# A gated FFN with a convolution over time: gate and up computed with tokens stationary instead of weights stationary

## The reference

```python
D_FF = 5632
def conv_ffn(h, w_up, conv_w, conv_b, w_down):
    s = h.shape[1]
    u = h @ w_up                                   # 256 x 2048 times 2048 x 11264
    u_pad = jnp.pad(u, ((0, 0), (CONV_WIDTH - 1, 0), (0, 0)))
    u = sum(conv_w[j] * u_pad[:, j:j + s] for j in range(CONV_WIDTH)) + conv_b
    gate, up = jnp.split(u, 2, axis=-1)
    return (jax.nn.silu(gate) * up) @ w_down       # 256 x 5632 times 5632 x 2048
```

## Time and profile before

| | |
|---|---|
| median of 3 runs | 2358.61 us |
| span of the profiled execution (its time less what lies around the span) | 2357.3 us |
| TensorE busy | 2348.9 us |
| VectorE busy | 1523.7 us |
| ScalarE busy | 1222.5 us |
| GpSimd busy | 364.5 us |
| HBM read | 446.54 MB, 190 GB/s over the span |

### The profile page before, as it was taken

How to read it: one execution, slowest core, us unless ns; L and a number is a source line. 1 busy time by engine, 2 the same in 40 slices (tenths; PEclk the granted TensorE clock), 3 DMA queues, 4 the chain that set the end, 5 groups by cost and what they waited for, 6 DMA issues and landing times.

```text
span 2357.3 us, 30238 instructions
## 1 busy us (share of the span) xinstructions
PE 2348.9 (100%) x11538; PEld 1988.3 (84%) x11538; DVE 1523.7 (65%) x1807; ACT 1222.5 (52%) x1598; POOL 364.5 (15%) x612
## 2 busy tenths in 40 slices
PE   9999999999999999999999999999999999999999
PEld 7998888888888888888877888888888888888887
DVE  6777865677567657667666676766655564565564
ACT  6555555555455445445565665655543443453442
POOL 0221410000000000000000445534231121130110
PEclk9999999999999999999999999999999999999999
DMA  9566786565655655655655767667676776766774
GB/s 307 166 188 178 162 218 210 166 189 183 210 179 184 208 180 185 208 180 179 223 191 164 212 196 220 200 213 218 199 222 202 198 212 206 203 207 206 204 217 150
DMA packets 310610, 468.10 MB, mean 199 GB/s; under 512 B 22577, under 2 KB 152241, under 8 KB 309825
## 3 DMA queue, kind: packets, MB, share of 16 engines
q1 hardware_dynamic: 291920, 440.52, 60.5%
q0 software_dynamic: 18016, 25.37, 5.0%
q10 hardware_dynamic: 528, 0.27, 0.1%
HBM read 446.54 MB, written 2.10 MB: 190 GB/s over the span
## 4 chain that ended last, share of the span: by engine, by line
PE 99%; DVE 0%; DMA 0%; SPq 0%; ACT 0%; issue 0%; POOL 0%; DVEq 0%
PE main L618 95%; PE aux L618 3%; PE aux L631 0%; DMA RAW<-in_w_in 0%; DVE LO L1260 0%; DVE AR L1263 0%; DVE XT L1263 0%; SPq L562 0%; PE aux L717 0%; SPq L575 0%; SPq L577 0%; PE aux L693 0%; DVE AR L1260 0%; ACT HI L864 0%; PE aux L641 0%
## 5 line engine op out<-in xcount | busy, mean ns | idle before, releaser
L1260 DVE TENSOR_TENSOR LO<-RAW,HI 128x1024 fp32r<-128x1024 f32 (+2 forms) x836 | 1011.4, 1229 | 630.2 <-ACT HI L864 604.0
L864 ACT ACTIVATE HI<-RAW 128x1024 fp32r<-128x1024 f32 (+2 forms) x836 | 853.6, 1043 | 684.2 <-PE main L618 586.0
L618 PE MATMUL main<-HI,XT 128*128 128x512 f32 (+1 forms) x2496 | 766.0, 385 | 2.6 <-DVE LO L1260 2.6
L618 PE MATMUL main<-HI,YT 128*128 128x512 f32 x2240 | 692.4, 389 | 0.0
L618 PEld LDWEIGHTS main<-HI,XT 128*128 128x128 f32 x2496 | 466.0, 188 | 94.3 <-issue 2.9
L618 PEld LDWEIGHTS main<-HI,YT 128*128 128x128 f32 x2240 | 420.4, 188 | 87.2
L618 PE MATMUL main<-LO,XT 128*128 128x512 f32 (+1 forms) x1248 | 479.1, 384 | 0.0
L618 PE MATMUL main<-XT,HI 128*128 128x512 f32 x1920 | 467.1, 392 | 0.0
L618 PE MATMUL main<-LO,YT 128*128 128x512 f32 x1120 | 435.7, 389 | 0.0
L618 PEld LDWEIGHTS main<-XT,HI 128*128 128x128 f32 x1920 | 350.9, 188 | 66.9 <-issue 0.2
L618 PEld LDWEIGHTS main<-LO,XT 128*128 128x128 f32 x1248 | 234.4, 188 | 43.9
(11 more groups left out here) (92 smaller groups left out, 839.4 us busy)
## 6 DMA issues: line engine op xcount, KB each, us to landing
RAW<-in_mlp_w SPq DMA_DIRECT2D x256, 512.0 KB, 4.0
RAW<-in_w_up SPq DMA_DIRECT2D x176, 512.0 KB, 4.8
RAW<-in_na_w_qkv SPq DMA_DIRECT2D x96, 512.0 KB, 4.9
RAW<-in_w_in SPq DMA_DIRECT2D x92, 512.0 KB, 4.7
RAW<-in_w_down SPq DMA_DIRECT2D x88, 512.0 KB, 5.0
RAW<-in_w_out SPq DMA_DIRECT2D x32, 512.0 KB, 4.4
RAW<-in_w_ple_gate SPq DMA_DIRECT2D x32, 512.0 KB, 4.6
RAW<-in_na_w_o SPq DMA_DIRECT2D x32, 512.0 KB, 4.6
```

The source lines that it names most:

```text
L618: return L.e.matmul(out, l, r, start=start, stop=stop, skip_group_check=True)
L864: return L.e.activation(out, x, f, **kw)
L1260: return L.e.tensor_tensor(out, x, y, op)
```

## The change

Gate and up become 22 blocks of form x, 512 channels and 8 slots each, so 176 slots as before. The blocks are numbered f: even ones are gate, odd ones up of the same channels. Down has three passes, over 16, 12 and 16 chunks (32, 24 and 32 slots, 88 as before), and one gate block is put ahead of each of the first two passes. The result of a block now has tokens on the partitions, so it must be turned:

- ScalarE copies the block out of PSUM, scaled by the token's norm factor (`evacuate`; HF shares its memory with AF, so a gate block's copy waits for the product of the pair before);
- VectorE turns it in squares of 32x32 into TBF (two instructions);
- GpSimd issues 16 transfers of 32 KB, TBF to TMF (`f_move`); for the last block 8 of them go to ScalarE's queue (`f_rest`);
- six slots behind the block ScalarE copies TMF into UB in token order (two instructions, and a small one for the tokens ahead of the first), and makes the tap with the bias (four) (`f_rows`);
- a slot later VectorE makes the other two taps (eight instructions, `f_taps`);
- silu, product and the split into YT follow at later slots (`f_silu`, `f_mult`, `f_split`).

The multiplication by RB and its making (`spread`, `rb`, DG) go, and so do `w_half`, `w_sum` and `two_parts` for these blocks. Three small loads of the start share one semaphore.

```diff
-FF_GROUPS = (12, 12, 10, 10)
+FF_GROUPS = (16, 12, 16)
@@ layout
-        for c in range(0, n, 2):
-            add("w", a["w_up"], (hc + c) * 128, 256, allk, "x", "gate", hc + c, c)
-            add("w", a["w_up"], D_FF + (hc + c) * 128, 256, allk, "x", "up", hc + c, c)
+        for i in range(hc // 4, (hc + n) // 4):
+            if grp == 0 or i > hc // 4:
+                add("x", a["w_up"], i * 512, 512, allk, "x", "gate", i)
+            add("x", a["w_up"], D_FF + i * 512, 512, allk, "x", "up", i)
+        if grp < 2:
+            add("x", a["w_up"], (hc + n) * 128, 512, allk, "x", "gate", (hc + n) // 4)
@@ stages
+    for f in range(22):
+        last = 159 + 8 * f + (0 if f < 9 else 32 if f < 15 else 56)
+        soon = f == 21
+        put(end, last, "f_move", f)
+        if soon:
+            put(mid, last + 1, "f_rest", f)
+        put(mid, last + (3 if soon else 6), "f_rows", f)
+        put(mid, last + (4 if soon else 7), "f_taps", f)
+        if f % 2 == 0:
+            put(mid, last + 9, "f_silu", f // 2)
+        else:
+            put(mid, last + (5 if soon else 8), "f_mult", f // 2)
+            put(mid, last + (5 if soon else 9), "f_split", f // 2)
@@ ScalarE
+            def f_rows(f):
+                A = AF[f % 2]
+                L.wait_ge(S("d_fu"), moved_ff(f + 1))
+                if f == 21:
+                    L.wait_ge(S("d_sc"), 144)
+                if f:
+                    L.wait_ge(S("v_cv"), 8 * f)
+                src = TMF.rearrange("p g (k t n) -> p t k g n", t=2, n=32)
+                dst = UB[:, :, 8:T + 8].rearrange("p k (t g n) -> p t k g n", t=2, n=32)
+                for t in range(2):
+                    act(dst[:, t], src[:, t], ACT.Copy)
+                before_first = UB[:, :, 0:8].rearrange("p k (c r) -> p k c r", r=4)[..., 1:4]
+                act(before_first, src[:, 1, :, 3, 24:32].rearrange("p k (c r) -> p k c r", r=4)[..., 0:3], ACT.Copy)
+                for m in range(4):
+                    ch = 4 * (f // 2) + m + (f % 2) * FFC
+                    act(A[:, m, :].rearrange("p (t g n) -> p t g n", t=2, n=32), src[:, :, m], ACT.Identity,
+                        scale=COL[:, P_CW + 176 + ch:P_CW + 176 + ch + 1], bias=COL[:, P_CB + ch:P_CB + ch + 1]).then_inc(S("a_cv"), 1)
@@ ScalarE, evacuate
+                elif k[0] in ("gate", "up"):
+                    f = ff_at(k)
+                    L.wait_ge(S("v_rs"), 2)
+                    if f > 1:
+                        L.wait_ge(S("v_gu") if f % 2 == 0 else S("v_tyl"), f // 2 if f % 2 == 0 else f - 1)
+                    for t in range(2):
+                        act(HF[f % 2][:, t, :], out[:, t, :], ACT.Copy, scale=rs[:, t:t + 1]).then_inc(S("a_fh"), 1)
@@ VectorE
+            def f_taps(f):
+                A = AF[f % 2]
+                L.wait_ge(S("g_pad"), 2)
+                for tap, off in ((1, 4), (0, 0)):
+                    for m in range(4):
...
+                            L.wait_ge(S("a_cv"), 4 * f + m + 1)
...
+                        stt(A[:, m, :], UB[:, m, off:off + T], COL[...], A[:, m, :], ALU.mult, ALU.add).then_inc(S("v_cv"), 1)
@@ VectorE, evacuate
+                elif k[0] in ("gate", "up"):
+                    f = ff_at(k)
+                    L.wait_ge(S("d_fu"), 256 * f)
+                    for t in range(2):
+                        L.wait_ge(S("a_fh"), 2 * f + t + 1)
+                        x = L.e.transpose(TBF..., HF[f % 2][:, t, :]...)
+                    x.then_inc(S("v_fb"), 1)
@@ GpSimd
+            def f_move(f):
+                L.wait_ge(S("v_fb"), f + 1)
+                L.wait_ge(S("a_cv"), 4 * f)
+                for p in range(2) if f == 21 else range(4):
+                    for d in range(4):
+                        L.e.dma_start(TMF[32 * d:32 * d + 32, p, :], TBF[32 * p:32 * p + 32, d, :]).then_inc(S("d_fu"), 16)
```

More of the change, by code:

```diff
@@ L471, in program @@
             paired.append(b.what)
-            if b.what == ("mix", 3) or b.what == ("down", 3, 3):
+            if b.what == ("mix", 3) or b.what == ("down", 2, 3):
                 paired.append(("e", 1 if b.what[0] == "mix" else 3))
@@ L478, in freed @@
         def freed(k):
-            if k[0] in ("hf", "hq", "qf", "kf", "gate", "up"):
+            if k[0] in ("hf", "hq", "qf", "kf"):
                 return "v_wy", wth[k] + 1
+            if k[0] in ("gate", "up"):
+                return "a_fh", 2 * ff_at(k) + 2
             if k[0] == "m1":
@@ L512, in stream, with ff_at, ff_slot, moved_ff @@
             return 8 * inst + (GATED.index((c, t)) if inst == 2 else 2 * c + t) + 1
-        def ff_at(hc, c, j):
-            return 2 * (hc // 2) + j, (c // 2) % 2
+        def ff_at(k):
+            return 2 * k[1] + (k[0] == "up")
+        wants = {k: freed(paired[i - 2]) for i, k in enumerate(paired) if i > 1}
         def half_of(b):
-            return (TMF if b.what[0] in ("gate", "up") else TMP)[wth[b.what] % 2]
+            return TMP[wth[b.what] % 2]
+        def ff_slot(i):
+            return 4 * (i if i < 4 else i - 4 if i < 7 else i - 7)
+        def moved_ff(n):
+            return 256 * n - 128 * (n // 22)
         def y_parts(i, t):
@@ L751, in spread @@
                 for t in range(2):
-                    x = mm(out[:, t * 128:t * 128 + 128], ones, (DG0, DG)[n][:, t, :], True, True)
+                    x = mm(out[:, t * 128:t * 128 + 128], ones, DG0[:, t, :], True, True)
                 x.then_inc(S("p_rb"), 1)
@@ L839, in tensor_engine @@
                     if b.kind == "w":
[L840 to L843, removed]
+                        w_high(b, j, cs, out)
                         w_low(b, j, cs, out)
@@ L1053, in rb @@
                 L.wait_ge(S("p_rb"), n + 1)
[L1054 to L1058, removed]
+                act(RB0, banks[bank["spread", n]][:, 0:256], ACT.Copy).then_inc(S("a_rb"), 1)
             def gate(t):
@@ L1963, in gpsimd_engine @@
                     load("d_gf", GP, row_bc(a["g_ffn_post"]))
-                elif k == ("gate", 0, 0):
+                elif k == ("gate", 0):
                     L.wait_ge(S("p_use"), b.last + 1)
-                    for w in U:
-                        for u in w:
-                            L.e.memset(u[:, :, 0:2], 0.0).then_inc(S("g_pad"), 1)
-                elif k == ("down", 3, 3):
+                    for c in (0, 4):
+                        L.e.memset(UB[:, :, c:c + 1], 0.0).then_inc(S("g_pad"), 1)
+                elif k == ("down", 2, 3):
                     L.wait_ge(S("v_acc"), 16)
                     load("d_gl", GP, row_bc(a["g_ple_post"]))
-                    L.wait_ge(S("p_rb"), 2)
+                    L.wait_ge(S("p_rb"), 1)
                     for h in range(NBI):
```

148 lines of the change are left out of this document (52 added, 96 removed).

## The result

The changed kernel took 2424.57 us, the median of 5 runs (2423.02 to 2425.49), beside 2359.16 us for the kernel before (5 runs, 2358.59 to 2359.66). The ratio is 1.0278, with a 95% interval from 1.0266 to 1.0289. The forecast was 2422 us in a range from 2385 to 2446.

What follows compares the result with a forecast made beforehand. The prediction took TensorE's matmuls to bound the kernel: 2357.3 - 11.0 - 0.5 + 61.2 (waits) + 11.6 (pauses) + 1.7 (clock) = 2420.3, plus 1.3 around the span, rounded to 2422 us. Range 2385 to 2446.

Steps and rivals of the forecast that it cites:

- Pace and token scales: Gate and up: fewer matmuls per slot save 11.0 us; dropping four token-scale matmuls before the second block saves 0.5 us.
- The loop: From one block's turns to the next: 24.2 us gate to up, 26.0 up to gate, against TensorE's 21.76.
- the three runs of blocks: FFN blocks 0 to 8, 9 to 14 and 15 to 21, with predicted waits 21.8, 12.7 and 26.7 us.
- The waits: TensorE in the FFN waits 61.2 us in all for the loop's overruns and the last block's tail.
- The pauses: GpSimd pauses during FFN transfer issues; two counted in full, 11.6 us, bounds 0 and 18.
- The clock: TensorE restarts at a lower clock behind the last block's wait of some 11 us, losing 1.7 us.
- Rival 1: FFN loop fits in 21.76 us or nearly, transfers about 9.2 us, only the tail waits: 2357 us; chance 0.07.
- Rival 2: VectorE and ScalarE overlap instructions, each loop step 1 to 1.5 us shorter: 2380 to 2395 us; chance 0.07.
- Rival 3: TensorE's clock falls with short waits too, beyond 2500 us if kept through a run; chance 0.04 together with worse pauses.

Runs made afterwards that it cites:

- e9: Changed kernel with HF in own memory, taps later, last down pass begun without the last block, that block's 16 transfers all on GpSimd: 2347.54 us.
- e11: Changed kernel with 12 of each block's 16 transfers (last block keeps all), unmoved squares read as zeros: 2390.61 us.
- e3: Changed kernel with 8 of each block's 16 transfers (last block keeps all), unmoved squares read as zeros: 2361.54 us.
- e5: Changed kernel with two added VectorE instructions, results unused, right behind each block's turns: 2424.66 us.
- e2: Changed kernel with HF alone given memory of its own, taps left where they were: 2410.77 us.

## Why the prediction was right, term by term

**Pace and token scales (-11.5): right.** e9 has the same matmuls as the changed kernel and waits as short as before: its span is 2357.3 - 2346.0 = 11.3 us shorter. The pace measured per slot was the right price: 11.0 us over 704 matmuls, 15.6 ns for each that went. The 13.3 ns that the prediction names beside it is what one matmul costs beyond its columns with tokens stationary; by it the gain would have been 9.4 us. The Trainium skill (TensorE: Matmul & The Clock Gate, "Wait — 56ns, not 53.3ns?") gives about 2.5 ns per warm matmul, an estimate of 1.8 us for the 704; the runs do not agree with it.

**The loop: right, in each leg.** From the rows above, predicted against measured: transfers from turns' end to read 12.5 / 13.2; rows 3.55 / 3.1; splits 2.3 / 2.2; taps 3.4 / 3.2; split 1.2 / 1.1; turns 1.3 / 1.3. Sum 24.25 / 24.2. The steps from up to gate, 26.0 predicted, are 25.42 to 27.60 in the first run of blocks, 26.4 on the average. The 4.8 us from last issue to read are 543.20 - (530.27 + 7.84 - 0.49) = 5.6 us here. The estimate of 2.1 us by the Trainium skill (DMA: Bandwidth & Descriptors, "Anatomy of one DMA") is farther off still.

**The waits (61.2): right as a sum, with the pauses in it.** TensorE's waits in the windows of the three runs of blocks are 21.0, then 11.1 + 2.2 = 13.3, then 18.0 + 9.2 = 27.2: 61.5 in all, against 21.8 + 12.7 + 26.7. The agreement is a little too good: the 61.5 hold what the pauses cost, so the steps alone gave some 55, an estimate that takes off 3.1 us for each pause.

**The pauses (11.6): mis-sized.** I took two in full. They showed 3.1 us each, 6 in all, where they fell between blocks, and e11 shows what two cost in the middle of one.

**What was missing: the restart.** This term was not in the sum at all. 39 waits of the FFN at 0.27 us are 10.5 us. The prediction summed waits as if a matmul row could stop and go free of charge.

**The clock (1.7): too small.** It fell three times, not once. Behind 705.30 ten matmuls took 3.98 us instead of 2.27, behind 1166.64 and 1180.27 seven took 3.1 instead of 1.6: 1.7 + 1.5 + 1.5 = 4.7 us, of which 0.3 is restart already counted. The 1.7 us of the prediction came from the slow first six passes of the kernel, which it put down to the lower level of the clock. The profile does not show that: its granted clock is 1.00 over the first 5 us of the kernel before. The 1.5 to 1.7 us measured for one dip agree with its figure all the same.

Together 61.5 + 10.5 + 4.4 = 76.4 us. The spans of the changed kernel and of e9 are 2423.7 - 2346.0 = 77.7 apart, and e9 waits 0.6 us in the FFN, so some 2 us stay without account. So the forecast of 2422 came within 3 us partly because a pause term of 11.6 us, half of which was too much and half of which already lies in the measured 61.5, stood in for restarts and clock that it lacked, 10.5 + 4.4 - 1.7 = 13.2 us. The mechanism and the steps were right; that the sum came so close is in part luck.

**Rivals.** Rival 1 needed a transfers' leg of about 9.2 us; e3, whose leg is 3.9 us shorter (9.3), has its time: 2361.5 where the rival's working gave 2357. The point from which it decides was placed well, and the changed kernel lies 4 us beyond it. Rival 2, shorter steps by overlap, is refuted by the steps; overlap is real (3.1 for 3.55, 3.2 for 3.4), but the transfers took back what it gave. Rival 3 did not happen in the changed kernel: behind the 36 shorter waits of the FFN, of at most 2.25 us, the clock stayed at 1.00. That was not to be relied on, since e5 has six dips behind waits of 2.01 to 2.60 us; there, as the rival's own working says of a lower level, they cost nothing.

**Open.** Why the gate-to-up steps of e2 are 0.3 to 0.5 us shorter, and why a pause inside a block is mostly longer than the 3.1 us that show between blocks.

## What to carry to other kernels

When a result goes round over several engines and queues and comes back to an engine that works in order, add up the round trip from one instruction to the same one of the next block and compare it with the block's time on the bounding engine; if it is longer, every block pays the difference, whatever the busy shares say. The cure is in the order, not in the work: let the next block's first step stand ahead of this block's last one (here 65 us for two slots and 2048 numbers of memory per partition). And put the last block's share behind all work that can do without it.

## What the runs showed of the hardware

- A stop of TensorE's row costs more than the wait named: 0.27 us (0.24 to 0.29 over 36 waits of the changed kernel), as 0.16 before the matmul's start and 0.11 to its successor.
- In the changed kernel the granted clock fell to 0.50 behind waits of 3.04, 4.13 and 9.21 us, each time for 3 to 4 us of work, and stayed at 1.00 through the 36 other waits of the FFN. The length of the wait before does not settle it: in e5 it fell behind waits of 2.01 to 2.60 us and stayed at 1.00 behind others of 2.57 and 3.11 us.
- GpSimd's pause between transfer issues comes every 128 issues whatever the block size (ahead of the 129th of the FFN with 8, 12, 14 and 16 per block, and of the 257th with 12, 14 and 16). Between blocks it showed 3.1 us whatever the idle time before; within a block it was 3.03 to 7.02 us.
